# RMS norms of a two-block transformer step: the root read straight from PSUM, and residual additions alternating with the scaled products

## The chip, the cores and the metric

One NeuronCore of one Trainium2 chip runs the whole program. The metric is the device time in microseconds (us) of one execution, as the median of several. The engines are TensorE (PE, matrix products; PEld its weight loads), VectorE (DVE), ScalarE (ACT), GpSimd (POOL) and SyncE (SP, which issues the loads). They run their own instruction lists and meet at semaphores.

## The reference, cut to what matters

Two blocks follow one another on an activation of 256 tokens by 2048 channels in fp32. The first block is attention and a state-space mixer (SSM) side by side, an output projection, and a feed-forward part; the second is a linear-attention mixer (RWKV) and grouped attention, an output projection, and a layer of experts. All of them are joined by norms over the channels:

```python
def rms_norm(x, w):
    xf = x.astype(jnp.float32)
    y = xf * lax.rsqrt(jnp.mean(xf * xf, axis=-1, keepdims=True) + NORM_EPS)
    return (y * w.astype(jnp.float32)).astype(x.dtype)

# first block
h = rms_norm(x, ln_mix_pre[l])
...                                   # mixer; inside it two norms of 512 channels each
x = x + rms_norm(mixed, ln_mix_post[l])
h = rms_norm(x, ln_ffn_pre[l])
...
x = x + rms_norm(f, ln_ffn_post[l])
# second block
h = rmsnorm(x, norm1_w[l])
...
x = x + jnp.concatenate([y_rwkv, y_attn], axis=-1) @ w_out[l]
h2 = rmsnorm(x, norm2_w[l])
x = x + peer_ffn(h2, w_pq[l], sub_keys[l], u_tab[l], v_tab[l])
return rmsnorm(x, normf_w)
```

## The kernel before, in words

Activations lie with channels on the 128 partitions and the 256 tokens along the row, so 2048 channels are 16 tiles of 128x256. `xT` holds the residual stream, `acc` the output of a projection, `h_two` the normed activation as two fp32r parts (`h_hi`, `h_lo`). Weights come as panels of 128 output channels (1 MB) into `raw`; ScalarE copies them to `w_hi`, VectorE subtracts to get `w_lo`, and TensorE multiplies: `chunk` issues, for each of the 16 tiles of the sum, a product with `w_hi` (L502) and one with `w_lo` (L504). These weight streams fill nearly the whole program. Between two streams stands a norm, and no product of the next stream can start before it.

A norm goes through four engines' lists, by helpers that are called nine times, at the places `mix_pre`, `ssm` (two halves), `mix_post`, `ffn_pre`, `ffn_post`, `norm1`, `norm2`, `normf`:

- ScalarE, `squares` (L1098): squares four tiles at a time, in groups 0 to 3, into `quad[g % 2]`. Group g waits for its source, and from group 2 on for the sums of group g-2 (`sq_summed`), since there are two `quad` buffers.
- TensorE, `sums` (L525; L654 for the SSM halves): a matrix of ones sums the squares over the channels into `bank[2]` in PSUM, four matmuls for each group (the records show eight, for fp32 goes in two passes).
- VectorE, `rstd` (L1537, L1540): one TENSOR_SCALAR reads the bank and writes mean plus epsilon to `rb[0]` (`ms_done`); it then waits for the root and takes the reciprocal into `rb[0]`.
- ScalarE, `rms` (L1103): the square root, `rb[0]` to `rb[1]` (`rms_done`).
- After it either `normed` (L1555) on VectorE with `h_upper` (L1108) on ScalarE and `h_lower` (L1545) on VectorE make `h_two`, or `renew` on VectorE does the residual: 16 products `acc * weight * rb[0]` (L1566), then four additions of four tiles each to `xT` (L1571), each of which signals `x_new`. The squares of the following norm wait for `x_new` group by group.

So `mix_post` is followed at once by `ffn_pre`, and `ffn_post` by `norm1`: squares, sums, root, products, additions, and again squares, sums, root, products. Each engine runs its list strictly in the order written; nothing is planned by a scheduler. In the SSM norm, TensorE sums half 0, then half 1 into the same `bank[2]`, and before the second it waits for `ms_done`, that is until VectorE has read the first. VectorE treats half 0 completely (root, products, `h_lower`), then half 1. TensorE meanwhile begins the output projection, whose tiles 8 to 11 and 12 to 15 wait for the `h_lower` of the halves.

Of the kernel before, what the change touches and what calls it, by code (L numbers as in the profile page):

```python
# [13 lines left out]
P = 128  # L14
# [171 lines left out]
def build(nc, a, out):  # L186
    with ExitStack() as ctx:
        def sb(name, shape, dt=F32, at=ctx):
            return at.enter_context(nc.sbuf_tensor(name, shape, dt))

        def sem(name):
            return ctx.enter_context(nc.semaphore(name))
# [10 lines left out]
        stage = [sb(f"stage{j}", [P, T]) for j in range(2)]  # L203
        quad = [sb(f"quad{j}", [P, 4, T]) for j in range(2)]
        rb = [sb(f"rb{j}", [P, T]) for j in range(2)]


        part = ExitStack()
# [103 lines left out]
        copied, drained, acc_upper = sem("copied"), sem("bank_drained"), sem("acc_upper_added")  # L312
        stage_used = sem("stage_used")
        sq_ready, sq_summed = sem("squares_ready"), sem("squares_summed")
        ms_done, rms_done, rstd_done = sem("ms_done"), sem("rms_done"), sem("rstd_done")
        quad_ready, h_hi_done, h_lo_done = sem("quad_ready"), sem("h_hi_done"), sem("h_lo_done")
        x_new, acc_done = sem("x_renewed"), sem("acc_scaled")
        relb_loaded, toep_done, toep_copied, bias_in = (
# [170 lines left out]
        def _(pe):  # L489
# [159 lines left out]
            for g in range(2):  # L649
                pe.wait_ge(sq_ready, SQ["ssm"] + g + 1)  # L650
                if g == 1:
                    pe.wait_ge(ms_done, RS["ssm"] + 1)
                for k in range(4):
                    last = nc.tensor.matmul(bank[2][:, 0:T], ones, quad[g][:, k, :], start=(k == 0), stop=(k == 3))  # L654
                last.then_inc(sq_summed, 1)
# [408 lines left out]
        def _(act):  # L1064
# [28 lines left out]
            def squares(src, first, ready, groups=4):  # L1093
                for g in range(groups):
                    ready(g)
                    if g >= 2:
                        act.wait_ge(sq_summed, first + g - 1)
                    nc.scalar.activation(quad[g % 2][:], src[:, 4 * g:4 * g + 4, :], ACT.Square  # L1098
                                         ).then_inc(sq_ready, 1)

            def rms(i):
                act.wait_ge(ms_done, i + 1)
                nc.scalar.activation(rb[1][:], rb[0][:], ACT.Sqrt).then_inc(rms_done, 1)  # L1103

            def h_upper(first, groups=4, tile0=0):
                for g in range(groups):
# [2 lines left out]
                                         ).then_inc(h_hi_done, 1)  # L1109

            squares(xT, SQ["mix_pre"], lambda g: act.wait_ge(s_x, 64))
            split(0, 0)
            rms(RS["mix_pre"])
            h_upper(HG["mix_pre"])
            split(1, 0)
            for h in range(HEADS1):
# [57 lines left out]
                act.wait_ge(y_gated, 4 * g + 4)  # L1174
                nc.scalar.activation(quad[g][:], proj[:, 32 + 4 * g:36 + 4 * g, :], ACT.Square).then_inc(sq_ready, 1)
            for g in range(2):
                rms(RS["ssm"] + g)
                act.wait_ge(quad_ready, HG["ssm"] + g + 1)
                nc.scalar.activation(h_hi[:, 8 + 4 * g:12 + 4 * g, :], quad[g][:], ACT.Copy).then_inc(h_hi_done, 1)
            plain(N_OUT1, DT, acc)  # L1180
            squares(acc, SQ["mix_post"], lambda g: act.wait_ge(drained, N_OUT1 + 4 * g + 4))
            rms(RS["mix_post"])
            squares(xT, SQ["ffn_pre"], lambda g: act.wait_ge(x_new, XG["mix_post"] + g + 1))
            rms(RS["ffn_pre"])
            h_upper(HG["ffn_pre"])


# [29 lines left out]
                for j in range(2):  # L1217
                    split(c + DT + j, it0)
            squares(acc, SQ["ffn_post"], lambda g: act.wait_ge(drained, N_IN2))
            rms(RS["ffn_post"])  # L1220
            squares(xT, SQ["norm1"], lambda g: act.wait_ge(x_new, XG["ffn_post"] + g + 1))
            rms(RS["norm1"])
            h_upper(HG["norm1"])
            with act.Fori(0, 15) as i:
                for j in range(2):
# [155 lines left out]
                nc.scalar.activation(h_hi[:, 2 * p:2 * p + 2, :], quad[p % 2][:, 2:4, :], ACT.Copy).then_inc(gn_hi, 1)  # L1381
            plain(N_OUT2, DT, acc)
            squares(xT, SQ["norm2"], lambda g: act.wait_ge(x_new, XG["mix2"] + g + 1))
            rms(RS["norm2"])
            for g in range(4):
                act.wait_ge(quad_ready, HG["norm2"] + g + 1)
                nc.scalar.activation(h_hi[:, 4 * g:4 * g + 4, :], h_f32[:, 4 * g:4 * g + 4, :], ACT.Copy
# [72 lines left out]
                for j in range(2):  # L1460
                    split(N_PEER + DT + j + 2, (g + 1) * DT + i)
            squares(xT, SQ["normf"], lambda g: act.wait_ge(x_new, XG["peer"] + g + 1))
            rms(RS["normf"])

        @block.gpsimd
        def _(pool):

            nc.gpsimd.memset(relb[32:33, :], NEG).then_inc(relb_set, 1)
            for h in range(HEADS1):

                pool.wait_ge(toep_copied, h + 1)
                pool.dma_start(toep_d[h:h + 1, 0:P * 512].rearrange("a (p n) -> (a p) n", n=512), toep[h % 2][:]
                               ).then_inc(toep_out[h % 2], 16)
            for j in range(2):
                pool.wait_ge(toep_out[j], 16 * (HEADS1 // 2))
            for h in range(HEADS1):
                skew = toep_d[h:h + 1, P:P + P * 511].rearrange("a (p n) -> (a p) n", n=511)
                pool.dma_start(bias[:, h, :], skew[:, 0:T]).then_inc(bias_in, 16)

            pool.wait_ge(qk_done, 5)  # L1480
            pool.dma_start(k_swap[0:64, :, :], proj2[64:128, 38:40, :]).then_inc(k_swapped, 16)
            pool.dma_start(k_swap[64:128, :, :], proj2[0:64, 38:40, :]).then_inc(k_swapped, 16)

            pool.wait_ge(s3_done, 8)
            nc.gpsimd.memset(acc[:], 0.0).then_inc(acc_zero, 1)
            for b in range(T // 16):
                pool.wait_ge(gates_copied, 8 * (b + 1))
# [12 lines left out]
        def _(dve):  # L1500
# [31 lines left out]
                    for j in range(2):  # L1532
                        add_lower(n0 + count - 2 + j, c0 + count - 1 + j, dst[:, count - 2 + j, :])

            def rstd(i, squares_end, width):
                dve.wait_ge(sq_summed, squares_end)
                nc.vector.tensor_scalar(rb[0][:], bank[2][:, 0:T], 1.0 / width, EPS, ALU.mult, ALU.add  # L1537
                                        ).then_inc(ms_done, 1)
                dve.wait_ge(rms_done, i + 1)
                nc.vector.reciprocal(rb[0][:], rb[1][:]).then_inc(rstd_done, 1)  # L1540
                dve.wait_ge(rstd_done, i + 1)
# [20 lines left out]
            def renew(weight, scaled0):  # L1562

                for g in range(4):
                    for k in range(4):
                        last = nc.vector.scalar_tensor_tensor(acc[:, 4 * g + k, :], acc[:, 4 * g + k, :],  # L1566
                                                              pc(weight, 4 * g + k), rb[0][:], ALU.mult, ALU.mult)
                    last.then_inc(acc_done, 1)
                for g in range(4):
                    dve.wait_ge(acc_done, scaled0 + g + 1)  # L1570
                    nc.vector.tensor_tensor(xT[:, 4 * g:4 * g + 4, :], xT[:, 4 * g:4 * g + 4, :],  # L1571
                                            acc[:, 4 * g:4 * g + 4, :], ALU.add).then_inc(x_new, 1)

            dve.wait_ge(s_par, 16)
            dve.wait_ge(s_x, 64)
            rstd(RS["mix_pre"], SQ["mix_pre"] + 4, D)
            normed(HG["mix_pre"], "ln_mix_pre")
            lower(0, 0)
            lower(1, 0)
# [138 lines left out]
                                    ).then_inc(y_gated, 1)  # L1718
            dve.wait_ge(y_gated, 8)
            for g in range(2):  # L1720
                rstd(RS["ssm"] + g, SQ["ssm"] + g + 1, D // 4)
                dve.wait_ge(sq_summed, SQ["ssm"] + g + 1)
                for k in range(4):
                    last = nc.vector.scalar_tensor_tensor(quad[g][:, k, :], proj[:, 32 + 4 * g + k, :],
                                                          pc("ssm_norm_w", 4 * g + k), rb[0][:], ALU.mult, ALU.mult)
                last.then_inc(quad_ready, 1)
                h_lower(HG["ssm"] + g, quad[g][:], 8 + 4 * g)
            drain_to(acc, N_OUT1, C_OUT1, DT)
            rstd(RS["mix_post"], SQ["mix_post"] + 4, D)
            renew("ln_mix_post", 0)  # L1730
            rstd(RS["ffn_pre"], SQ["ffn_pre"] + 4, D)
            normed(HG["ffn_pre"], "ln_ffn_pre")


# [69 lines left out]
                    gather_down(i, FQT)  # L1804
                gather_down(DT // 2 - 1, DT)
            dve.wait_ge(drained, N_IN2)
            rstd(RS["ffn_post"], SQ["ffn_post"] + 4, D)
            renew("ln_ffn_post", 5)
            rstd(RS["norm1"], SQ["norm1"] + 4, D)
            normed(HG["norm1"], "norm1")  # L1810


# [315 lines left out]
            for g in range(4):  # L2128
                nc.vector.tensor_tensor(xT[:, 4 * g:4 * g + 4, :], xT[:, 4 * g:4 * g + 4, :],
                                        acc[:, 4 * g:4 * g + 4, :], ALU.add).then_inc(x_new, 1)  # L2130
            rstd(RS["norm2"], SQ["norm2"] + 4, D)
            for g in range(5):
                if g < 4:
                    for k in range(4):
# [168 lines left out]
            rstd(RS["normf"], SQ["normf"] + 4, D)  # L2303
            for g in range(4):
                if g >= 2:
                    dve.wait_ge(out_stored[g % 2], 16)
# [91 lines left out]
```

## Time and profile before

| | us |
|---|---|
| median of 3 runs | 3956.2 (3951.4 to 3966.77) |
| the profiled execution, time | 3949.75 |
| the profiled execution, span | 3948.1 |
| TensorE matmuls busy | 3589.8 (91%) |
| VectorE busy | 2446.9 (62%) |
| ScalarE busy | 1571.2 (40%) |

Mean granted TensorE clock over the span: 0.942 of full speed. Times in rows are us from the start of the span, durations marked "mean ns" are nanoseconds. A timeline row gives start, length, engine, line, operation, output<-inputs and, in brackets, how long the engine sat idle before it and what ended that. Rows of the same form that follow each other are merged, with their count behind the x. An engine idle for a time is free of charge unless it is on the chain that sets the end.

### The profile page before, as it was taken

The page shows a single profiled execution, that of the slowest core. Times are in us where ns is not written, and L with a number is a line of the kernel's source. Part 1 is how long each engine was busy: PE and PEld are TensorE (multiplying, and loading weights), DVE is VectorE, ACT ScalarE, POOL GpSimd, SP SyncE. Part 2 cuts the span into 40 slices and gives each one's busy share as a digit, 9 for nine tenths or more (in the row PEclk, how much of TensorE's full clock was granted, in tenths as well). Part 3 has the DMA queues.
Part 4 walks back from the last instruction along what each step waited for, and adds up shares of the span by engine and source line. Part 5 has one row for each costly group of instructions (what it writes and reads, how often), then busy time and mean ns, then how long its engine had stood idle before and what let it go on. Part 6 is the DMA issues. An engine that isn't in the chain of part 4 may idle for free.

```text
span 3948.1 us, 71481 instructions
## 1 busy us (share of the span) xinstructions
PE 3589.8 (91%) x24910; PEld 3057.9 (77%) x24910; DVE 2446.9 (62%) x4140; ACT 1571.2 (40%) x2433; POOL 32.7 (1%) x47
## 2 busy tenths in 40 slices
PE   6996979999999799568886898899999999999998
PEld 5884768888888688337775787688888888888887
DVE  3464567676767676536654559965656555565665
ACT  3433334444444344223322331443544444444543
POOL 0000000000000000000000000100000000000000
PEclk8996989999999999658998999999999999999999
DMA  4551225555555355000011453556656565656653
GB/s 171 187 182 43 100 102 182 190 174 195 173 195 173 130 187 192 23 6 13 8 35 39 142 167 122 174 180 211 212 181 213 184 213 185 212 182 212 202 189 130
DMA packets 165674, 593.36 MB, mean 150 GB/s; under 512 B 18432, under 2 KB 26752, under 8 KB 164288
## 3 DMA queue, kind: packets, MB, share of 16 engines
q1 hardware_dynamic: 159600, 559.10, 42.8%
q0 software_dynamic: 5968, 32.77, 2.3%
q8 instruction: 76, 1.25, 0.1%
q14 instruction: 30, 0.25, 0.0%
HBM read 572.66 MB, written 18.87 MB: 150 GB/s over the span
## 4 chain that ended last, share of the span: by engine, by line
PE 82%; DVE 12%; ACT 3%; issue 2%; DMA 1%; DVEq 0%; SPq 0%; ACTq 0%; POOL 0%; POOLq 0%
PE bank L502 46%; PE bank L504 24%; PE bank L754 5%; PE bank L525 2%; DVE hot_row L2234 1%; PE bank L742 1%; PE bank L716 1%; DVE hot_col L2229 1%; DVE quad L1555 1%; DVE proj L2003 0%; ACT w_hi L1070 0%; PE bank L732 0%; DVE q_ms L1865 0%; DVE h_two L1545 0%; DVE rb L1540 0%
## 5 line engine op out<-in xcount | busy, mean ns | idle before, releaser
L502 PE MATMUL bank<-h_two,w_hi 128*128 128x512 f32 x5616 | 1968.5, 395 | 44.2 <-DVE h_two L1545 30.3
L504 PE MATMUL bank<-h_two,w_lo 128*128 128x256 f32 x5616 | 1575.9, 281 | 0.0
L1505 DVE TENSOR_TENSOR w_lo<-raw,w_hi 128x1024 fp32r<-128x1024 f32 (+1 forms) x1054 | 1224.7, 1185 | 223.3 <-ACT w_hi L1070 217.8
L502 PEld LDWEIGHTS bank<-h_two,w_hi 128*128 128x128 f32 x5616 | 1057.7, 188 | 291.3 <-issue 37.9
L1070 ACT ACTIVATE w_hi<-raw 128x1024 fp32r<-128x1024 f32 (+1 forms) x1054 | 1045.2, 1025 | 562.7 <-PE bank L504 520.0
L504 PEld LDWEIGHTS bank<-h_two,w_lo 128*128 128x128 f32 x5616 | 1066.3, 190 | 0.0
L502 PE MATMUL bank<-p_two,w_hi 128*128 128x512 f32 x1792 | 631.0, 395 | 3.1 <-DVE acc L1523 1.9
L504 PE MATMUL bank<-p_two,w_lo 128*128 128x256 f32 x1792 | 500.7, 279 | 0.0
L502 PEld LDWEIGHTS bank<-p_two,w_hi 128*128 128x128 f32 x1792 | 336.5, 188 | 87.5 <-DVE p_two L2248 5.6
L504 PEld LDWEIGHTS bank<-p_two,w_lo 128*128 128x128 f32 x1792 | 336.5, 188 | 0.0
L1519 DVE TENSOR_TENSOR acc<-acc,bank 128x256 f32 x192 | 81.0, 422 | 393.2 <-PE bank L504 393.1
L1075 ACT ACTIVATE stage<-bank 128x256 f32<-128x256 f32 x242 | 93.0, 384 | 479.2 <-PE bank L504 478.8
L502 PE MATMUL bank<-f_two,w_hi 128*128 128x512 f32 x704 | 250.3, 397 | 12.0 <-DVE f_two L1771 12.0
L1515 DVE TENSOR_TENSOR stage<-stage,bank 128x256 f32<-128x256 f32 x242 | 101.9, 421 | 206.7 <-ACT stage L1075 206.5
L504 PE MATMUL bank<-f_two,w_lo 128*128 128x256 f32 x704 | 200.6, 285 | 0.0
L502 PEld LDWEIGHTS bank<-f_two,w_hi 128*128 128x128 f32 x704 | 134.8, 192 | 41.8 <-DVE f_two L1771 13.2
L504 PEld LDWEIGHTS bank<-f_two,w_lo 128*128 128x128 f32 x704 | 135.9, 193 | 0.0
L999 PE MATMUL bank<-h_f,raw 128*128 128x256 f32 x512 | 120.5, 381 | 0.0
L525 PE MATMUL bank<-quad,cst 128*128 128x256 f32 x224 | 62.9, 450 | 50.7 <-ACT quad L1098 50.7
L999 PEld LDWEIGHTS bank<-h_f,raw 128*128 128x128 f32 x512 | 93.6, 192 | 10.4
L525 PEld LDWEIGHTS bank<-quad,cst 128*128 128x128 f32 x224 | 51.0, 231 | 61.9 <-ACT quad L1098 41.1
L1036 PEld LDWEIGHTS bank<-hot_row,hot_col 128*128 128x128 f32 x512 | 68.0, 206 | 38.2 <-DVE hot_row L2234 35.1
(328 smaller groups left out, 2850.6 us busy)
## 6 DMA issues: line engine op xcount, KB each, us to landing
raw<-in_u_tab SPq DMA_DIRECT2D x256, 512.0 KB, 4.0
raw<-in_v_tab SPq DMA_DIRECT2D x256, 512.0 KB, 4.5
raw<-in_w_up SPq DMA_DIRECT2D x176, 512.0 KB, 4.8
raw<-in_w_in SPq DMA_DIRECT2D x174, 512.0 KB, 4.3
raw<-in_w_out SPq DMA_DIRECT2D x64, 512.0 KB, 4.5
raw<-in_w_down SPq DMA_DIRECT2D x64, 512.0 KB, 3.5
raw<-in_w_pq SPq DMA_DIRECT2D x32, 512.0 KB, 4.4
gates<-g_stage POOLq DMA_DIRECT2D x16, 896.0 KB, 5.3
```

The source lines that it names most:

```text
L502: nc.tensor.matmul(o[:], wh, two[:, k, :, :].rearrange("p a t -> p (a t)"), start=(k == 0), stop=False)
L504: last = nc.tensor.matmul(o[:, T:2 * T], wl, two[:, k, 0, :], start=False, stop=(k == nk - 1))
L525: last = nc.tensor.matmul(bank[2][:, 0:T], ones, quad[g % 2][:, k, :], start=(g == 0 and k == 0), stop=(g == groups - 1 and k == 3))
L716: last = nc.tensor.matmul(bank[3 + qh % 2][:, tt * T:(tt + 1) * T], proj2[r:r + 64, 30 + m, tt * P:(tt + 1) * P], k_t, start=True, stop=True)
L754: return nc.tensor.matmul(o, lhs, rhs, start=start, stop=stop)
L999: last = nc.tensor.matmul(bank[c % 2][:, 0:T], raw[c % 2][:, k * P:(k + 1) * P], h_f32[:, k, :], start=(k == 0), stop=(k == DT - 1))
L1036: last = nc.tensor.matmul(bank[3 + n % 2][:, x * P:(x + 1) * P], hot_col[n % 2][:, x, :], hot_row[n % 2][:, x, :], start=True, stop=True)
L1070: nc.scalar.activation(w_hi[c % 2][:, at:end], raw[c % 2][:, at:end], ACT.Copy).then_inc(hi_done, 1)
L1075: nc.scalar.activation(dst, bank[c % 2][:, 0:T], ACT.Copy).then_inc(copied, 1)
L1505: nc.vector.tensor_tensor(w_lo[c % 2][:, at:end], raw[c % 2][:, at:end], w_hi[c % 2][:, at:end].bitcast(F32), ALU.subtract).then_inc(lo_do ...
L1515: nc.vector.tensor_tensor(dst, dst, bank[c % 2][:, T:2 * T], ALU.add).then_inc(drained, 1)
L1519: nc.vector.tensor_tensor(dst, dst, bank[c % 2][:, 0:T], ALU.add).then_inc(acc_upper, 1)
```

## The change

ScalarE takes the root from PSUM with `scale=1/width` and `bias=eps`, where `eps` is a new tile of 128x1, filled once by GpSimd at the start. VectorE's TENSOR_SCALAR goes, and `ms_done` with it. ScalarE now waits for the sums itself, and for the previous reciprocal, which read `rb[1]`. TensorE's wait in the SSM norm is for the root of half 0 instead of its mean. In `renew` the addition of a group follows the four products of that group. The other calls change in their arguments alone.

```diff
+        eps = sb("eps", [P, 1])
...
                 if g == 1:
-                    pe.wait_ge(ms_done, RS["ssm"] + 1)
+                    pe.wait_ge(rms_done, RS["ssm"] + 1)
...
-            def rms(i):
-                act.wait_ge(ms_done, i + 1)
-                nc.scalar.activation(rb[1][:], rb[0][:], ACT.Sqrt).then_inc(rms_done, 1)
+            def rms(i, squares_end, width=D):
+
+                act.wait_ge(sq_summed, squares_end)
+                if i:
+                    act.wait_ge(rstd_done, i)
+                nc.scalar.activation(rb[1][:], bank[2][:, 0:T], ACT.Sqrt, scale=1.0 / width, bias=eps[:]
+                                     ).then_inc(rms_done, 1)
...
             squares(xT, SQ["mix_pre"], lambda g: act.wait_ge(s_x, 64))
+            act.wait_ge(eps_set, 1)
             split(0, 0)
-            rms(RS["mix_pre"])
+            rms(RS["mix_pre"], SQ["mix_pre"] + 4)
...
         def _(pool):
 
+            nc.gpsimd.memset(eps[:], EPS).then_inc(eps_set, 1)
+            pool.wait_ge(eps_set, 1)
             nc.gpsimd.memset(relb[32:33, :], NEG).then_inc(relb_set, 1)
...
-            def rstd(i, squares_end, width):
-                dve.wait_ge(sq_summed, squares_end)
-                nc.vector.tensor_scalar(rb[0][:], bank[2][:, 0:T], 1.0 / width, EPS, ALU.mult, ALU.add
-                                        ).then_inc(ms_done, 1)
+            def rstd(i):
                 dve.wait_ge(rms_done, i + 1)
                 nc.vector.reciprocal(rb[0][:], rb[1][:]).then_inc(rstd_done, 1)
                 dve.wait_ge(rstd_done, i + 1)
...
                     last.then_inc(acc_done, 1)
-                for g in range(4):
                     dve.wait_ge(acc_done, scaled0 + g + 1)
                     nc.vector.tensor_tensor(xT[:, 4 * g:4 * g + 4, :], xT[:, 4 * g:4 * g + 4, :],
                                             acc[:, 4 * g:4 * g + 4, :], ALU.add).then_inc(x_new, 1)
...
             for g in range(2):
-                rstd(RS["ssm"] + g, SQ["ssm"] + g + 1, D // 4)
-                dve.wait_ge(sq_summed, SQ["ssm"] + g + 1)
+                rstd(RS["ssm"] + g)
```

## Rows read from the trace of the kernel before

**Rows 1.** The page: busy time of PE, and the chain that ended last.
```profile
PE 3589.8 (91%) x24910; PEld 3057.9 (77%) x24910; DVE 2446.9 (62%) x4140; ACT 1571.2 (40%) x2433; POOL 32.7 (1%) x47
PE 82%; DVE 12%; ACT 3%; issue 2%; DMA 1%; DVEq 0%; SPq 0%; ACTq 0%; POOL 0%; POOLq 0%
```
**Rows 2.** Timeline from mix_post's root to ffn_pre's: start, us, engine, line, operation.
```profile
535.17 0.42 DVE L1537 TENSOR_SCALAR rb<-bank 128x256 f32<-128x256 f32 x1 [9.37 <-PE bank L525]
535.63 0.42 ACT L1103 ACTIVATE rb<-rb 128x256 f32<-128x256 f32 x1 [2.80 <-DVE rb L1537]
536.08 1.75 DVE L1540 RECIPROCAL rb<-rb 128x256 f32<-128x256 f32 x1 [0.48 <-ACT rb L1103]
537.86 6.42 DVE L1566 SCALAR_TENSOR_TENSOR acc<-acc,par,rb 128x256 f32<-128x256 f32 x16
544.20 4.63 DVE L1571 TENSOR_TENSOR xT<-xT,acc 128x1024 f32<-128x1024 f32 x4
545.46 2.20 ACT L1098 ACTIVATE quad<-xT 128x1024 f32<-128x1024 f32 x2 [9.41 <-DVE xT L1571]
...
546.57 9.41 PE L525 MATMUL bank<-quad,cst 128*128 128x256 f32 x32 [11.44 <-ACT quad L1098]
550.45 1.06 ACT L1098 ACTIVATE quad<-xT 128x1024 f32<-128x1024 f32 x1 [2.80 <-PE bank L525]
...
556.02 0.42 DVE L1537 TENSOR_SCALAR rb<-bank 128x256 f32<-128x256 f32 x1 [7.19 <-PE bank L525]
```
**Rows 3.** Granted clock: us from:to, busy of PE, PEld, DVE, ACT, POOL, PEclk, DMA.
```profile
548.50:550.50 2.00, 2.00 (x6) 1.63 (x5) 0.33 (x1) 0.05 (x1) 0.00 (x0) 0.50 0.00 0
552.50:554.50 2.00, 2.00 (x11) 1.77 (x10) 0.00 (x0) 1.06 (x1) 0.00 (x0) 1.00 0.00 0
```
**Rows 4.** Timeline of ffn_post and norm1, the same two norms again.
```profile
1325.33 1.28 ACT L1103 ACT_TABLE_LOAD   x1
1327.74 0.42 DVE L1537 TENSOR_SCALAR rb<-bank 128x256 f32<-128x256 f32 x1 [7.30 <-PE bank L525]
...
1336.77 4.62 DVE L1571 TENSOR_TENSOR xT<-xT,acc 128x1024 f32<-128x1024 f32 x4
...
1348.25 0.42 DVE L1537 TENSOR_SCALAR rb<-bank 128x256 f32<-128x256 f32 x1 [6.86 <-PE bank L525]
```
**Rows 5.** Timeline of the norm in the SSM, in two halves.
```profile
416.61 1.99 PE L654 MATMUL bank<-quad,cst 128*128 128x256 f32 x8
...
418.71 0.42 DVE L1537 TENSOR_SCALAR rb<-bank 128x256 f32<-128x256 f32 x1 [1.05 <-PE bank L654]
418.76 1.28 ACT L1103 ACT_TABLE_LOAD   x1
...
419.28 1.97 PE L654 MATMUL bank<-quad,cst 128*128 128x256 f32 x8 [0.68 <-DVE rb L1537]
...
426.23 0.42 DVE L1537 TENSOR_SCALAR rb<-bank 128x256 f32<-128x256 f32 x1
...
426.46 0.47 PE L502 MATMUL bank<-h_two,w_hi 128*128 128x512 f32 x1 [2.44 <-DVE h_two L1545]
...
427.13 1.75 DVE L1540 RECIPROCAL rb<-rb 128x256 f32<-128x256 f32 x1 [0.48 <-ACT rb L1103]
```
**Rows 6.** The first norm, mix_pre, on ScalarE.
```profile
20.23 1.28 ACT L1103 ACT_TABLE_LOAD   x1
...
21.52 0.42 ACT L1103 ACTIVATE rb<-rb 128x256 f32<-128x256 f32 x1
```
**Rows 7.** The nine roots: duration ns min/median/max, first and last start.
```profile
L1103 ACT ACTIVATE rb<-rb x9: 416/416/418, 21.5 to 3935.0; 128x256 f32<-128x256 f32 x9
```
**Rows 8.** Groups by line and form in 1765 to 1850 us: busy us, mean ns.
```profile
L1291 ACT ACTIVATE sig_a<-bank,small 128x256 f32<-128x256 f32 x6 | 2.5, 471 | 8.5 <-PE bank L765 8.5
```
**Rows 9.** The page's costliest groups: products on the tiles that lie behind `eps`.
```profile
L502 PE MATMUL bank<-p_two,w_hi 128*128 128x512 f32 x1792 | 631.0, 395 | 3.1 <-DVE acc L1523 1.9
...
L502 PE MATMUL bank<-f_two,w_hi 128*128 128x512 f32 x704 | 250.3, 397 | 12.0 <-DVE f_two L1771 12.0
```

More of the change, by code:

```diff
@@ L314, in build @@
         sq_ready, sq_summed = sem("squares_ready"), sem("squares_summed")
[L315 removed]
+        eps_set, rms_done, rstd_done = sem("eps_set"), sem("rms_done"), sem("rstd_done")
         quad_ready, h_hi_done, h_lo_done = sem("quad_ready"), sem("h_hi_done"), sem("h_lo_done")
@@ L1176, in _ @@
             for g in range(2):
-                rms(RS["ssm"] + g)
+                rms(RS["ssm"] + g, SQ["ssm"] + g + 1, D // 4)
                 act.wait_ge(quad_ready, HG["ssm"] + g + 1)
@@ L1181, in _ @@
             squares(acc, SQ["mix_post"], lambda g: act.wait_ge(drained, N_OUT1 + 4 * g + 4))
-            rms(RS["mix_post"])
+            rms(RS["mix_post"], SQ["mix_post"] + 4)
             squares(xT, SQ["ffn_pre"], lambda g: act.wait_ge(x_new, XG["mix_post"] + g + 1))
-            rms(RS["ffn_pre"])
+            rms(RS["ffn_pre"], SQ["ffn_pre"] + 4)
             h_upper(HG["ffn_pre"])
@@ L1219, in _ @@
             squares(acc, SQ["ffn_post"], lambda g: act.wait_ge(drained, N_IN2))
-            rms(RS["ffn_post"])
+            rms(RS["ffn_post"], SQ["ffn_post"] + 4)
             squares(xT, SQ["norm1"], lambda g: act.wait_ge(x_new, XG["ffn_post"] + g + 1))
-            rms(RS["norm1"])
+            rms(RS["norm1"], SQ["norm1"] + 4)
             h_upper(HG["norm1"])
@@ L1383, in _ @@
             squares(xT, SQ["norm2"], lambda g: act.wait_ge(x_new, XG["mix2"] + g + 1))
-            rms(RS["norm2"])
+            rms(RS["norm2"], SQ["norm2"] + 4)
             for g in range(4):
@@ L1462, in _ @@
             squares(xT, SQ["normf"], lambda g: act.wait_ge(x_new, XG["peer"] + g + 1))
-            rms(RS["normf"])
+            rms(RS["normf"], SQ["normf"] + 4)
         @block.gpsimd
         def _(pool):
+            nc.gpsimd.memset(eps[:], EPS).then_inc(eps_set, 1)
+            pool.wait_ge(eps_set, 1)
             nc.gpsimd.memset(relb[32:33, :], NEG).then_inc(relb_set, 1)
@@ L1575, in _ @@
             dve.wait_ge(s_x, 64)
-            rstd(RS["mix_pre"], SQ["mix_pre"] + 4, D)
+            rstd(RS["mix_pre"])
             normed(HG["mix_pre"], "ln_mix_pre")
@@ L1728, in _ @@
             drain_to(acc, N_OUT1, C_OUT1, DT)
-            rstd(RS["mix_post"], SQ["mix_post"] + 4, D)
+            rstd(RS["mix_post"])
             renew("ln_mix_post", 0)
-            rstd(RS["ffn_pre"], SQ["ffn_pre"] + 4, D)
+            rstd(RS["ffn_pre"])
             normed(HG["ffn_pre"], "ln_ffn_pre")
@@ L1806, in _ @@
             dve.wait_ge(drained, N_IN2)
-            rstd(RS["ffn_post"], SQ["ffn_post"] + 4, D)
+            rstd(RS["ffn_post"])
             renew("ln_ffn_post", 5)
-            rstd(RS["norm1"], SQ["norm1"] + 4, D)
+            rstd(RS["norm1"])
             normed(HG["norm1"], "norm1")
@@ L2130, in _ @@
                                         acc[:, 4 * g:4 * g + 4, :], ALU.add).then_inc(x_new, 1)
-            rstd(RS["norm2"], SQ["norm2"] + 4, D)
+            rstd(RS["norm2"])
             for g in range(5):
@@ L2302, in _ @@
                                         acc[:, 4 * g:4 * g + 4, :], ALU.add).then_inc(x_new, 1)
-            rstd(RS["normf"], SQ["normf"] + 4, D)
+            rstd(RS["normf"])
             for g in range(4):
```

## The prediction

> **What bounds the kernel now.** I read the page's busy times and its chain first. TensorE is busy 91% of the span and holds 82% of the chain that ended last; VectorE has 12% and ScalarE 3% [rows 1]. So the time is set by weight streams, and nothing that the change edits lies inside a stream. What it edits are the nine norms between the streams, where TensorE waits and VectorE, ScalarE and TensorE hand one tile to and fro. The second view is therefore the timeline of one such stretch, from the root of mix_post to that of ffn_pre [rows 2]. The reader is to see that it is one serial chain: each engine's idle time in brackets is ended by the engine before it in the chain, so each step taken out there should come off the total. The third view is the granted clock in that stretch [rows 3], because TensorE has idled 11.44 us before these sums. The fourth is the same timeline at the second pair of norms [rows 4], in the SSM [rows 5] and at the start [rows 6], because a table load or another queue may be the later of two waits there.
>
> **The root read straight from PSUM, at six plain norms** (mix_post, ffn_pre, ffn_post, norm1, norm2, normf). Removed: VectorE's operation that turns sums into mean plus epsilon. From its start to the start of the root it is 535.63 - 535.17 = 0.46 us [rows 2]. Added: the root now reads PSUM, takes a scale and a bias tile. The root takes 416 ns in all nine places [rows 7]. The nearest row to the new form is a Tanh of the same 128x256, from PSUM, with a scale and a bias tile: 471 ns [rows 8]. I take that: 55 ns more. The gain is 0.46 - 0.055 = 0.405 us each, six times 2.43 us. Bounds: at 416 ns it is 0.46 each, 2.8 in all. Whether ScalarE wakes as fast after TensorE as VectorE did no row here separates; VectorE took 418.71 - 418.60 = 0.11 us after the end of the sums [rows 5], and if ScalarE took twice that, the gain would be 0.3 each, 1.8 in all.
>
> The Trainium skill, in "ScalarE: Activation LUTs", section "What ACT_TABLE_LOAD costs", speaks against this edit: it says that a 128x1 pointer operand adds about 93 ns to an ACTIVATE. An estimate by that page, for six norms, would be 0.46 - 0.093 = 0.37 each and 2.2 in all. The Tanh row's 55 ns over the root is on the cheaper side of it; they differ in source as well, so it doesn't settle the rule.
>
> ScalarE's table load for the root must not be uncovered by this. At ffn_post it runs from 1325.33 to 1326.61 while ScalarE waits, and VectorE's operation begins only at 1327.74 [rows 4]; normf has the same order. The load is 1.13 us early, so the root can start at the end of the sums.
>
> **mix_pre.** Here the load is the later one: it begins at 20.23, ends at 21.51, and the root starts at 21.52 [rows 6], long after the sums. Taking VectorE's operation away gives nothing, and the root is 0.055 longer: -0.06 us. GpSimd's fill of `eps` is queued ahead of its first fill of `relb`, at the very start, 20 us before the root needs it; the copy of weights that waits for it comes after three rounds of squares and sums. I cost both at nothing; the cover is these 20 us.
>
> **The SSM norm.** Half 0: ScalarE's load, 418.76 to 420.04, ends after VectorE's operation (418.71 + 0.42 = 419.13) [rows 5], so here too the root starts when it did; the 0.055 that it is longer stays. TensorE's sums of half 1 began at 419.28, right after VectorE had read the bank; now they wait for the end of the root, about 420.05 + 0.47 = 420.52, so they come 1.24 us later. Queued behind them on TensorE are tiles 0 to 7 of the output projection. But tile 8 sat idle for 2.44 us before it started, for `h_lower` of half 0 [rows 5]. 1.24 of these 2.44 are eaten and 1.2 are left: cost nothing, with the cover named; without it the cost would be 1.24. Half 1: VectorE read the bank at 426.23, only after it was through with half 0, and the reciprocal came at 427.13. Now ScalarE makes the second root while VectorE is in `h_lower`, since nothing else is queued on it there, and the reciprocal follows `h_lower` directly: 427.13 - 426.23 = 0.90 us less 0.06 from half 0, so 0.84 us. That is on the path, for tiles 12 to 15 wait for it.
>
> Together: 2.43 - 0.06 + 0.84 = 3.21 us.
>
> **Residual additions between the products.** Before, the 16 products run from 537.86, then the four additions from 544.20 to 544.20 + 4.63 = 548.83. The first `x_new` thus comes late, the squares start at 545.46, and TensorE's four groups of sums follow each other until 556.02 [rows 2]. They are slow at first: from the start at 546.57 to the square that the first group released at 550.45 it is 3.88 us, at granted clock 0.50, the lower of the two levels (1.2 GHz); later it is 1.00 (2.4 GHz) [rows 3]. After the change the first group's products end at about 537.86 + 6.42/4 + 0.06 = 539.5, its addition at 540.8, its square at 541.9, and TensorE starts at 541.9 instead of 546.57. The low-clock groups then run beside VectorE's remaining products and additions, one group every 2.8 us or so. What is late next is VectorE's last addition. VectorE does the same work plus four waits for its own result. Such a wait costs the overlap of two operations, 537.86 + 6.42 - 544.20 = 0.08, and the handoff, 537.86 - (536.08 + 1.75) = 0.03 [rows 2]: 0.11 each, 0.44 in all. So the last addition ends at 549.27; 0.04 later its square, which takes 1.06, 0.05 to TensorE, and then one group of sums from rest at full clock, 418.71 - 416.61 = 2.10 us to the next engine's start [rows 5]: 552.52. Against 556.02 that is 3.50 us.
>
> At the second place the same sum gives 1336.77 + 4.62 + 0.44 + 0.04 + 1.06 + 0.05 + 2.10 = 1345.08 against 1348.25 [rows 4]: 3.17 us. Both: 6.67 us. This rests on the clock having risen by the last group. In rows 3 it rose 4 to 6 us after the sums had begun; that would be at 546 to 548 now, before the last square's end at 550.4. norm2 and normf have additions without products, so nothing is gained there but the root.
>
> **Sum.** 3.21 + 6.67 = 9.9 us, from 3949.75 to 3939.9 for the profiled execution, 0.25%. That execution is 6.5 us below the median of the runs shown, 3956.2; I take the gain off the median: 3946.3 us.
>
> **The rivals.** (a) The clock doesn't rise in time, and TensorE's sums become the bound of the interleaved stretch. At the low level four groups take 4 x 3.88 = 15.5 us from 541.9, to 557.4, which is 1.4 us later than before; likewise at the second place from about 1334.5 to 1350.0, 1.8 us later. The time would be 3956.2 - 3.2 + 3.2 = 3956. For it: these sums start after long idleness and come in pieces. Against: at the low clock a group takes 3.88 us and VectorE delivers one every 2.8, so TensorE would have no pause, and in the same sums before it rose after 4 to 6 us.
>
> (b) The root's table load slips behind the wait for the sums, because the root now has two waits. It is then uncovered at ffn_post and normf: 2 x 1.28 = 2.6 us, so 3948.9. Against: of two waits the added one, for the last reciprocal, was met long before. The Trainium skill, same page and section, says that a switch costs another 1380 ns of drain; an estimate by it would be 5.3 us for the two loads. The trace doesn't show that drain: the root starts 0.01 us after the load's end [rows 6].
>
> (c) Slower: `eps` is placed ahead of all tiles of the later parts, so `f_two`, `p_two`, `acc` and others move to other addresses. If reads from the new ones are slower, the long streams pay. The products on these two tiles that are in the rows sum to 631.0 + 250.3 = 881.3 us [rows 9]. They decide against the change from 9.9/881.3 = 1.1% on, 4.4 ns of each 395; at 13 ns more each (3.4%) it is 30 - 9.9 = 20 us slower, 3976. For it: nothing in the trace. Against: 395 and 397 ns on two tiles that lie at different places.
>
> (d) The change doesn't do what it says: the additions alternate but squares still go one by one behind TensorE; that is (a) in effect.
>
> **How the numbers follow.** Chances: forecast 0.76, (a) with its milder forms 0.10, (b) 0.08, (c) 0.04, something else 0.02. The unknown costs (0.3 to 0.46 a norm, the group of sums at either clock, 1 us of clock phase at each of three stream starts) give 6 to 12 us of gain. The three runs lie 15 us apart, so a median can be off by some 8. The range: 3936 to 3960. Over 0.5% (19.8 us), about what a measurement of this kernel can tell from no change, is twice the forecast gain: faster 0.06, within 0.89, slower 0.05.
>
> **What would show it.** In the changed kernel: a root of about 471 ns, with VectorE's L1537 gone; the reciprocal some 0.9 us earlier in SSM half 1; TensorE's sums of ffn_pre and norm1 starting 4 to 5 us earlier relative to the products and the root there following 3 to 3.5 us earlier; the streams with unchanged durations. It would be wrong if these sums end at the low clock, if a table load stands between the sums and the root, or if L502 changes its mean.

## The result, and the profile after

The changed kernel is slower, by 0.22%: ratio to the kernel before 1.0022, 95% interval 1.0012 to 1.0032, medians 3963.74 and 3955.07 us over 22 runs each. The forecast was 3946.3 with a range up to 3960; the time is 3.7 us above it, and on the other side of the kernel before. The profiled execution took 3954.64 us (span 3952.8).

The norms did what was forecast. The timeline of VectorE from mix_post's reciprocal to ffn_pre's, which answers [rows 2]:

```profile
529.35 1.75 DVE L1545 RECIPROCAL rb<-rb 128x256 f32<-128x256 f32 x1 [9.92 <-ACT rb L1107]
531.14 1.67 DVE L1571 SCALAR_TENSOR_TENSOR acc<-acc,par,rb 128x256 f32<-128x256 f32 x4
532.85 1.23 DVE L1575 TENSOR_TENSOR xT<-xT,acc 128x1024 f32<-128x1024 f32 x1
533.99 1.67 DVE L1571 SCALAR_TENSOR_TENSOR acc<-acc,par,rb 128x256 f32<-128x256 f32 x4
...
541.38 1.23 DVE L1575 TENSOR_TENSOR xT<-xT,acc 128x1024 f32<-128x1024 f32 x1
546.28 1.75 DVE L1545 RECIPROCAL rb<-rb 128x256 f32<-128x256 f32 x1 [3.68 <-ACT rb L1107]
```

Products and additions alternate, and from reciprocal to reciprocal it is 546.28 - 529.35 = 16.93 us, against 556.02 - 535.17 = 20.85 before [rows 2]. ScalarE and TensorE in the same stretch:

```profile
528.85 0.47 ACT L1107 ACTIVATE rb<-bank,eps 128x256 f32<-128x256 f32 x1 [2.34 <-PE bank L526]
534.11 1.06 ACT L1099 ACTIVATE quad<-xT 128x1024 f32<-128x1024 f32 x1 [4.79 <-DVE xT L1575]
...
542.64 1.06 ACT L1099 ACTIVATE quad<-xT 128x1024 f32<-128x1024 f32 x1 [1.78 <-DVE xT L1575]
545.78 0.47 ACT L1107 ACTIVATE rb<-bank,eps 128x256 f32<-128x256 f32 x1 [2.08 <-PE bank L526]
```
```profile
535.22 5.10 PE L526 MATMUL bank<-quad,cst 128*128 128x256 f32 x16 [6.41 <-ACT quad L1099]
540.91 1.99 PE L526 MATMUL bank<-quad,cst 128*128 128x256 f32 x8 [0.59 <-ACT quad L1099]
543.75 1.99 PE L526 MATMUL bank<-quad,cst 128*128 128x256 f32 x8 [0.85 <-ACT quad L1099]
```

The last two groups of sums wait for ScalarE, which waits for VectorE's addition: so VectorE's additions now set the time of this stretch. The clock, us from:to with PEclk (granted share of the full clock) behind POOL's busy time, rose some 3 us after the sums had begun:

```profile
536.00:538.00 2.00, 2.00 (x7) 1.53 (x6) 2.00 (x4) 1.05 (x1) 0.00 (x0) 0.50 0.00 0
538.00:540.00 2.00, 2.00 (x11) 1.71 (x9) 1.97 (x4) 0.22 (x2) 0.00 (x0) 0.99 0.00 0
```

Where did the time go? The start of the same matmul in both traces, taken every 250 matmuls, tells where they drift apart. After less before, in us: 0.0 at 90 us; -4.1 at the end of the first stream (312 us); -6.4 before mix_post; -10.55 after ffn_pre; -2.4 at the end of the feed-forward part; -6.3 after norm1 and up to norm2; -4.1 where the expert part's first p_two stream begins (2672 us); **+7.5** at its end; +5.1 at the last matmul, behind `normf`. So the norms gave what they should, and the long weight streams, where the change edits nothing, took some 8 us in the feed-forward part and 12 in the expert part. Of the 2.4 us that `normf` gave back, the root is only 0.4; its 32 sums, which the change leaves alone, ran in 7.17 us at a granted clock of 1.00, and in 10.03 us at first at 0.50 in the kernel before, which is luck of these two executions. The sums of `normf`, before and after:

```profile
3924.52 10.03 PE L525 MATMUL bank<-quad,cst 128*128 128x256 f32 x32 [3.32 <-ACT quad L1098]
```
```profile
3932.46 7.17 PE L526 MATMUL bank<-quad,cst 128*128 128x256 f32 x32 [3.32 <-ACT quad L1099]
```

The groups of the page, answering [rows 1] and [rows 9]:

```profile
PE 3606.0 (91%) x24910; PEld 3060.4 (77%) x24910; DVE 2443.8 (62%) x4131; ACT 1572.2 (40%) x2433; POOL 32.8 (1%) x48
...
L503 PE MATMUL bank<-h_two,w_hi 128*128 128x512 f32 x5616 | 1981.5, 398 | 39.3 <-DVE h_two L1550 25.1
...
L503 PE MATMUL bank<-p_two,w_hi 128*128 128x512 f32 x1792 | 631.4, 394 | 2.8 <-DVE acc L1531 1.7
...
L503 PE MATMUL bank<-f_two,w_hi 128*128 128x512 f32 x704 | 256.4, 405 | 11.8 <-DVE f_two L1774 11.8
```

TensorE has the same 24910 matmuls and is busy 16.2 us longer. The products on `f_two` grew from 250.3 to 256.4. The page's mean mixes stream starts at the low clock with the middle of the stream, so I cut windows inside streams: groups by form in 100 to 200 us (`h_two`), 890 to 930 (`f_two`) and 2780 to 2820 (`h_two` between two `p_two` streams). First the kernel before, then the changed one:

```profile
L502 PE MATMUL bank<-h_two,w_hi 128*128 128x512 f32 x284 | 100.4, 399 | 0.0
...
L502 PE MATMUL bank<-f_two,w_hi 128*128 128x512 f32 x117 | 40.6, 390 | 0.0
...
L502 PE MATMUL bank<-h_two,w_hi 128*128 128x512 f32 x116 | 40.3, 391 | 0.0
```
```profile
L503 PE MATMUL bank<-h_two,w_hi 128*128 128x512 f32 x290 | 100.6, 391 | 0.0
...
L503 PE MATMUL bank<-f_two,w_hi 128*128 128x512 f32 x114 | 40.3, 396 | 0.0
...
L503 PE MATMUL bank<-h_two,w_hi 128*128 128x512 f32 x114 | 40.3, 399 | 0.0
```

The reader is to see two paces of the same instruction at the same full clock (granted 1.00 in all six windows): 290 against 284 pairs of products in 100 us. From start to start within a stream a pair (one product with `w_hi`, one with `w_lo`) on `h_two` takes 346.7 ns or 353.3 ns, 1.9% apart, and it keeps one of them for a whole stream. Over all 8112 pairs that would be worth some 53 us. Of the streams compared here, the kernel before had the slow pace in the first one, the changed kernel in all four passes over `f_two` and in all eight `h_two` streams of the expert part. (The last of these eight holds the final group's expert values, which the kernel writes into `h_two`.)

It isn't a collision with the other engines' accesses. In the slow first stream of the kernel before, from 100 to 300 us, three pairs in a row always take 1060 ns: in 17 such triples during which ScalarE and VectorE were both busy for less than a tenth of the time as in 11 during which both were for more than nine tenths, and in 5 with no DMA under way as in 148 with more than twenty.

### The profile page after: what moved, and what is told of

Its sections match the earlier page's. It is cut to its first block, busy times and chain, and to the rows that moved or that the text cites. A ratio compares the mean times of both kernels' runs of the same rounds, so it can differ in the third digit from the quotient of the medians.

```text
span 3952.8 us, 71480 instructions
## 1 busy us (share of the span) xinstructions
PE 3606.0 (91%) x24910; PEld 3060.4 (77%) x24910; DVE 2443.8 (62%) x4131; ACT 1572.2 (40%) x2433; POOL 32.8 (1%) x48
## 4 chain that ended last, share of the span: by engine, by line
PE 82%; DVE 12%; ACT 3%; issue 2%; DMA 1%; DVEq 0%; SPq 0%; ACTq 0%; POOL 0%; POOLq 0%
PE bank L503 47%; PE bank L505 24%; PE bank L755 5%; DVE hot_row L2237 1%; PE bank L526 1%; PE bank L743 1%; PE bank L717 1%; DVE hot_col L2232 1%; DVE proj L2006 0%; PE bank L733 0%; ACT w_hi L1071 0%; DVE quad L1560 0%; DVE q_ms L1868 0%; DVE rb L1545 0%; PE bank L1037 0%
## 5 line engine op out<-in xcount | busy, mean ns | idle before, releaser
L503 PE MATMUL bank<-f_two,w_hi 128*128 128x512 f32 x704 | 256.4, 405 | 11.8 <-DVE f_two L1774 11.8
L1442 ACT ACTIVATE u_act<-stage 128x256 f32 x112 | 46.8, 418 | 124.7 <-DVE p_raw L2245 124.7
```

The source lines that it names most:

```text
L503: nc.tensor.matmul(o[:], wh, two[:, k, :, :].rearrange("p a t -> p (a t)"), start=(k == 0), stop=False)
L1442: nc.scalar.activation(tile_of(u_act, i * 2 + j), stage[j][:], ACT.Gelu).then_inc(gelu_done, 1)
```

## The experiments

Theory A: the pace depends on where the tiles lie. Tiles are allocated at multiples of 32 bytes, so `eps`, 4 bytes a partition, had pushed `proj`, `acc`, `f_two`, `p_two` and all else behind it 32 bytes on. Theory B: each stream falls into a pace by chance, so the 0.22% is bad luck in many draws. Places below are bytes past a multiple of 128, with the weight buffers at 0 unless said otherwise; a tile of `h_two`, `f_two` or `p_two` is 2048 bytes from the next, so the whole stream has the same place. The places are worked out from the order and sizes of the tiles in each kernel; the traces hold no addresses. Before: `h_two` 0, `f_two` 32, `p_two` 96. Changed: 0, 64, 0. A pace without a fence is the mean distance from start to start, in ns a pair, over that tile's streams in the trace.

**x1, one unused tile in the kernel before.**
```diff
         rb = [sb(f"rb{j}", [P, T]) for j in range(2)]
+        sb("pad", [P, 1])
```


> The kernel before with one unused tile of 128x1 ahead of the later parts, nothing else, so that proj, acc, f_two, p_two and the rest start 32 bytes further on. Theory A (addresses set the pace of the streams): products on f_two take the slow pace, 353.3 ns for a pair of products instead of 346.7, those on p_two some 352 instead of 351, and the h_two streams between the p_two streams turn slow as well; together about 4.7 + 2.0 + 12.7 = 19 us, ratio 1.004 to 1.005. Theory B (each stream falls into one of the two paces by chance at its start, whatever the addresses): ratio 0.999 to 1.001, and the paces of this profile are another mixture.

Measured: 1.0039 [1.0026, 1.0052], median 3975.07. `f_two` 353.3 in three of four passes, 349.1 in the last; `p_two` 351.1; all `h_two` streams between them 353.3, as theory A had it. An unused tile, with no instruction, costs more than the whole change. Windows 2700 to 2740 and 2780 to 2820:
```profile
L503 PE MATMUL bank<-p_two,w_hi 128*128 128x512 f32 x115 | 40.4, 393 | 0.0
...
L503 PE MATMUL bank<-h_two,w_hi 128*128 128x512 f32 x115 | 40.7, 399 | 0.0
```

**x2, the changed kernel with no tile moved.**
```diff
-        par = sb("par", [P, NPAR])
+        par_eps = sb("par", [P, NPAR + 1])
+        par, eps = par_eps[:, 0:NPAR], par_eps[:, NPAR:NPAR + 1]
-        eps = sb("eps", [P, 1])
```


> The changed kernel with eps in a spare column behind the parameters, so that no tile moves against the kernel before. Theory A: the gain of the norms stays alone, ratio 0.997 to 0.998 (about -10 us), and f_two at 346.7 ns a pair. Theory B: as the changed kernel, 1.001 to 1.003. Theory C (the changed order itself costs it somewhere in the streams): also 1.001 to 1.003, with f_two slow in places.

Measured: 0.9969 [0.9956, 0.9982], median 3943.21, which is 3.1 us below the forecast's 3946.3. `f_two` 346.8 to 347.4. Of the expert part's eight `h_two` streams the first, at 2565 us, ran at 353.3, the seven behind a `p_two` stream at 346.7. Windows 890 to 930 and 2780 to 2820:
```profile
L503 PE MATMUL bank<-f_two,w_hi 128*128 128x512 f32 x117 | 40.6, 390 | 0.0
...
L503 PE MATMUL bank<-h_two,w_hi 128*128 128x512 f32 x117 | 40.6, 391 | 0.0
```
x1 and x2 speak for A and against B as the cause of the 0.22%.

**x3, the kernel before with `h_two` at 32.**
```diff
+        sb("pad0", [P, 1])
         h_two = sb("h_two", [P, DT, 2, T], F32R)
+        sb("pad1", [P, 1])
```


> The kernel before with h_two moved by 32 bytes and everything from proj on by 64, so that h_two too starts at 32 bytes past a multiple of 64, as f_two and p_two do in the kernel before. Theory A in its simplest form (32 past a multiple of 64 is the fast place): all h_two streams at 346.7 ns a pair, ratio 0.998 to 1.0. Theory B: 0.999 to 1.001 with a mixture of paces.

Measured: 0.9972 [0.996, 0.9984], 3946.12, a little more gain than the 0.998 to 1.0 expected. All `h_two` streams at 346.7; `p_two`, which came to 32 by this, 346.7 too; `f_two`, which came to 96, 350.3. So it isn't the place within 64 bytes that counts, as I had written, but within 128: 32 and 96 differ.

**x4, the changed kernel again.** No edit.

> The changed kernel once more, for the repeat of its paces. Theory A: f_two slow in all four passes and the streams from 2660 us on slow, as in its first profile; ratio 1.002. Theory B: another mixture of paces.

Measured: 1.0013 [1.0002, 1.0024]. `f_two` at 353 in all passes, as the first time. Of the expert part's `h_two` streams the seven behind a `p_two` stream ran at 353.3 again, but the first, at 2574 us, at 346.7. And the streams of norm1 (672 pairs) and of the output projection behind it (256 pairs) ran at 353.3 this time and 346.7 the first: with `h_two` at 0 part of it is chance, as B says.

**x5, every moving tile at 32, in the changed kernel.**
```diff
+        sb("pad0", [P, 8])
         h_two = sb("h_two", [P, DT, 2, T], F32R)
+        sb("pad1", [P, 24])
...
         slot_T = sb("slot_T", [P, 3, T], at=part)
+        sb("pad2", [P, 16], at=part)
```
(on x2.)

> The changed kernel with eps in the spare column, and unused tiles that place h_two, f_two and p_two all at 32 bytes past a multiple of 128, the place at which every stream seen so far ran at 346.7 ns a pair. Theory A (addresses): all streams at 346.7; from the kernel before that is about -10 us of the norms, -6.4 us on the first h_two streams, -5.9 us on p_two (1792 pairs, 350.0 to 346.7): ratio 0.993 to 0.9955. Theory B (chance): as the run with tiles left in place, 0.9965 to 0.9975.

Measured: 0.9937 [0.9922, 0.9953], median 3929.45, the fastest kernel here. Every stream runs at 346.7 to 346.8. TensorE's busy time fell from 3606.0 to
```profile
PE 3574.5 (91%) x24910; PEld 3069.3 (78%) x24910; DVE 2444.1 (62%) x4131; ACT 1571.5 (40%) x2433; POOL 32.8 (1%) x48
```
Its six runs lie within 5.1 us (3926.06 to 3931.12), the 23 of the kernel before on the same chip within 19.8 (3945.11 to 3964.86). That would fit a draw of paces in the one and none in the other, but the same kernel's next six runs (x10) lie 14.9 us apart, one of them at 3938.66 and the others within 5.7, so the spread proves little.

**x6 and x7, the two parts of the change alone**, no tile moved.
```diff
 # x6, on the kernel before
                     last.then_inc(acc_done, 1)
-                for g in range(4):
                     dve.wait_ge(acc_done, scaled0 + g + 1)
 # x7, on x2
                     last.then_inc(acc_done, 1)
+                for g in range(4):
                     dve.wait_ge(acc_done, scaled0 + g + 1)
```


> The kernel before with only the additions put between the products. From mix_post's reciprocal to ffn_pre's it takes 20.85 us before and 16.93 in the changed kernel; theory of the forecast: the order alone brings it to 17.3 (0.4 more than the whole change, for the root), TensorE's sums start 4 to 5 us earlier; ratio 0.998 to 0.9987. Rival (VectorE's waits for its own results cost more than 0.11 each, or the clock stays low): over 18.5, ratio 0.999 or more.

> The kernel before with only the root from PSUM, eps in the spare column, additions behind all products as before. Forecast: 0.4 us off each of six norms, 0.84 us off the SSM norm, 3.2 us in all, ratio 0.999 to 0.9995; from mix_post's reciprocal to ffn_pre's 20.45 us. Rival (the root from PSUM saves nothing): 20.85 and ratio 1.0.

Measured: x6 0.9988 [0.9974, 1.0002], x7 0.9993 [0.9979, 1.0006]. Neither interval excludes 1, and both fit the forecast; with `h_two` at 0 the paces' draw hides gains of this size. The traces are sharper. VectorE from root to root in x6, then in x7:
```profile
535.65 1.75 DVE L1540 RECIPROCAL rb<-rb 128x256 f32<-128x256 f32 x1 [0.48 <-ACT rb L1103]
...
552.98 1.75 DVE L1540 RECIPROCAL rb<-rb 128x256 f32<-128x256 f32 x1 [0.48 <-ACT rb L1103]
```
```profile
526.34 1.75 DVE L1545 RECIPROCAL rb<-rb 128x256 f32<-128x256 f32 x1 [8.82 <-ACT rb L1107]
...
546.46 1.75 DVE L1545 RECIPROCAL rb<-rb 128x256 f32<-128x256 f32 x1 [7.36 <-ACT rb L1107]
```
x6: 17.33 us, expected 17.3. x7: 20.12, expected 20.45, and the missing 0.3 is in the sums, whose 32 matmuls took 9.08 us instead of 9.41 [rows 2] because the clock rose sooner, some 3.9 us after their start instead of 4.6. The gains of the two parts, 3.52 and 0.73 us, add up to 4.25, the whole change gave 3.92; they agree but for that 0.3.

**x8, the kernel before with `h_two` at 64**, the others where they were within 128 bytes.
```diff
+        sb("pad0", [P, 16])
         h_two = sb("h_two", [P, DT, 2, T], F32R)
+        sb("pad1", [P, 16])
```

> The kernel before with h_two at 64 bytes past a multiple of 128; f_two and p_two keep their places within 128 bytes. If the place within 128 bytes sets the pace for h_two as it did for f_two (353.1 ns at 64), the h_two streams are at 353; if only the place within 64 counts, they fall into 346.7 or 353.3 as they do at 0.

Measured: 3975.44 in one run, beside 3956.03. `h_two` never at 346.7: 349 or 353.3. `f_two`, at 32, ran at 346.7 to 347.0 between them. `p_two`, at 96 as in the kernel before, ran at 353.3 in six streams and at 346.7 in one, where it had had 350.0. So 128 bytes don't say it all. Taken within 256 bytes, `p_two` has moved here, from 96 to 224.

**x9 and x10, the change by itself with the paces held.** x9 is the kernel before with the pads of x5; x10 is x5 again, on the same chip.
```diff
 # x9, on the kernel before
+        sb("pad0", [P, 8])
         h_two = sb("h_two", [P, DT, 2, T], F32R)
+        sb("pad1", [P, 24])
...
+        sb("pad2", [P, 16], at=part)
```

> The kernel before, with h_two, f_two and p_two at 32 bytes past a multiple of 128 as in the best kernel, and nothing else changed. Theory A: all streams at 346.7, 12.3 us less than the kernel before in its first profile: ratio 0.996 to 0.9975. The best kernel over this one is then the change by itself with the paces held: 0.9970 to 0.9978 (9 to 12 us). Rival (the change gains nothing but lucky paces): both at the same time.

> The best kernel again, on the same chip as the kernel before with placed tiles: ratio 0.993 to 0.9955 to the kernel before, all streams at 346.7 again if addresses decide, a mixture if chance does.

Measured: x9 0.9963 [0.995, 0.9977], 3939.99; x10 0.9935 [0.9919, 0.9951], 3927.71. All streams of both at 346.7 to 347.4. The change is thus worth 3939.99 - 3927.71 = 12.3 us by the medians of six runs each (a ratio of 0.9969, where 0.9970 to 0.9978 was expected), 9.8 us by the profiled spans (3936.3 and 3926.5); the forecast was 9.9.

**x11 and x12, one tile each moved away from 32**, on x5.
```diff
 # x11: f_two to 64
+        sb("pad3", [P, 8], at=part)
         f_two = sb("f_two", [P, FQT, 2, T], F32R, at=part)
 # x12: p_two (and u_act, g_now with it) to 0
-        sb("pad2", [P, 16], at=part)
+        sb("pad2", [P, 8], at=part)
```


> The best kernel with f_two alone moved to 64 bytes past a multiple of 128, its place in the changed kernel. Theory A: only the f_two streams slow, 353 a pair, 704 x 6.6 ns = 4.6 us. Rival (a slow f_two drags the h_two streams behind it): h_two after f_two slow too.

> The best kernel with the expert part's tiles from u_act on moved so that p_two starts at a multiple of 128, its place in the changed kernel; h_two stays well placed. If h_two's slow pace between the p_two streams in the changed kernel was inherited from p_two but needs h_two's own place at 0 as well: p_two at 351, h_two at 346.7. If it is inherited regardless: h_two at 353.3 too, some 15 us in all.

Measured, one run each: 3933.01 and 3933.38. x11: `f_two` 353.2 to 353.4, everything else 346.7, and 4.7 us more than x10's profiled run, for 4.6 expected. The rival (a slow `f_two` drags `h_two`) falls for an `h_two` at 32. For one at 0 the changed kernel, x1 and x4 answer it: of the nine `h_two` streams that follow a slow `f_two` stream there, eight ran at 346.7. x12: `p_two` at 353.3 in four streams and at 347.0 in three; `h_two` 346.7 throughout. The 351 expected for `p_two` was missed: it had been at 0 within 128 bytes in the changed kernel as well, but at 128 within 256, and is at 0 within 256 here. So in the changed kernel the expert part's `h_two` could be slow behind `p_two` only because it lay at 0 itself. Windows of x11 at 890 to 930 and of x12 at 2700 to 2740 and 2780 to 2820:
```profile
L507 PE MATMUL bank<-f_two,w_hi 128*128 128x512 f32 x112 | 39.6, 397 | 0.0
```
```profile
L506 PE MATMUL bank<-p_two,w_hi 128*128 128x512 f32 x115 | 40.7, 399 | 0.0
...
L506 PE MATMUL bank<-h_two,w_hi 128*128 128x512 f32 x116 | 40.3, 390 | 0.0
```

**x13 and x14, weights moved too.** So far the weight buffers lay at 0 in every kernel, so a tile's place and its distance from the weights were the same number.
```diff
 # both, on x5
+        sb("pad_w", [P, 8])
         raw = [sb(f"raw{j}", [P, PW]) for j in range(2)]
 # x13 alone: keeps the moving tiles at 32; x14 has them at 64
-        sb("pad0", [P, 8])
```


> The best kernel with the weight buffers (raw, w_hi, w_lo) moved by 32 bytes as well, so that weights and moving tiles both start at 32 past a multiple of 128, where before the weights were at 0. Absolute theory (the moving tile's own address counts): all streams at 346.7 ns a pair, 3925 to 3930 us. Relative theory (the distance between moving tile and weights counts, 32 being the fast one): as at distance 0, p_two slow at 351 or more and h_two at 346.7 or 353.3, 3935 to 3955 us.

> Weights at 32 and h_two, f_two, p_two at 64 past a multiple of 128, so the distance is 32 again. Absolute theory: f_two at 353.1 as in the changed kernel, h_two 349 to 353.3 as in the run with h_two at 64, 3950 to 3975 us. Relative theory: all streams at 346.7, 3925 to 3930 us.

Measured: x13 3948.79, x14 3930.63, one run each. x13, with the moving tiles at 32 and distance 0, is no longer fast: `f_two` 351, `h_two` and `p_two` at either pace. x14, which is x5 with all tiles 32 bytes further on, has the moving tiles at 64, where they were slowest, and yet has every stream at 346.7 to 346.8, because the distance is 32. The absolute theory falls in both, the relative one holds in both (x14 is 0.6 us above its 3925 to 3930). The weights' three kinds of buffer, `raw`, `w_hi` and `w_lo`, moved together, and `xT` with them, so which of them counts isn't shown. Windows 2700 to 2735 and 2780 to 2820, x13 and then x14:
```profile
L506 PE MATMUL bank<-p_two,w_hi 128*128 128x512 f32 x101 | 35.7, 399 | 0.0
...
L506 PE MATMUL bank<-h_two,w_hi 128*128 128x512 f32 x114 | 40.3, 399 | 0.0
```
```profile
L507 PE MATMUL bank<-p_two,w_hi 128*128 128x512 f32 x102 | 35.4, 390 | 0.0
...
L507 PE MATMUL bank<-h_two,w_hi 128*128 128x512 f32 x117 | 40.6, 390 | 0.0
```

## Why the prediction was right or wrong, point by point

**The root, six norms: right.** The root takes 473 ns (median of nine) where 471 was taken from the Tanh row, and VectorE's operation is gone. The reciprocal of norm2 comes 15.26 us after the stream's last product, 15.67 before: 0.41 for a forecast 0.405. The Trainium skill's 93 ns for a 128x1 operand ("ScalarE: Activation LUTs", section "What ACT_TABLE_LOAD costs") isn't borne out as a sum here: 473 - 416 = 57 ns, with the source changed from SBUF to PSUM at the same time, so the operand alone remains unmeasured.

**The table load, rival (b): it stayed covered.** At ffn_post, ScalarE:
```profile
1323.07 1.28 ACT L1107 ACT_TABLE_LOAD   x1
1325.39 0.47 ACT L1107 ACTIVATE rb<-bank,eps 128x256 f32<-128x256 f32 x1 [1.04 <-PE bank L526]
```
The load ends at 1324.35, and ScalarE still waits 1.04 us for the sums.

**The SSM norm: the gain right, the cover gone where it was sought.** ScalarE, VectorE and TensorE in the changed kernel:
```profile
414.41 0.47 ACT L1107 ACTIVATE rb<-bank,eps 128x256 f32<-128x256 f32 x1
...
419.44 0.46 ACT L1107 ACTIVATE rb<-bank,eps 128x256 f32<-128x256 f32 x1
```
```profile
414.98 1.75 DVE L1545 RECIPROCAL rb<-rb 128x256 f32<-128x256 f32 x1 [2.98 <-ACT rb L1107]
...
420.71 1.75 DVE L1545 RECIPROCAL rb<-rb 128x256 f32<-128x256 f32 x1
```
```profile
410.96 1.99 PE L655 MATMUL bank<-quad,cst 128*128 128x256 f32 x8
415.03 3.62 PE L655 MATMUL bank<-quad,cst 128*128 128x256 f32 x8 [2.08 <-ACT rb L1107]
...
426.57 0.79 PE L503 MATMUL bank<-h_two,w_hi 128*128 128x512 f32 x1 [3.73 <-DVE h_two L1550]
```
And tile 12 in the kernel before:
```profile
432.99 0.79 PE L502 MATMUL bank<-h_two,w_hi 128*128 128x512 f32 x1 [4.89 <-DVE h_two L1545]
```
The second root runs beside `h_lower`, and the reciprocals are 5.73 us apart; before, from 420.50 to 427.13, 6.63. That is 0.90 less. From the start of the first sums to tile 12 it was 432.99 - 416.61 = 16.38 us and is 426.57 - 410.96 = 15.61, so the gain is 0.77 for a forecast 0.84. TensorE's sums of half 1 wait for the first root as written. They also run at the low clock for most of their time (3.62 us for 1.97 before [rows 5]), which I hadn't forecast. With that the 1.2 us of cover that I had left before tile 8 are gone: tile 8 no longer waits for `h_lower` of half 0, it comes 0.49 us after its end (421.29 after 420.80). This costs nothing only because tile 12 has a wait of its own, 4.89 us before and 3.73 now, which I hadn't named.

**The additions between the products: right.** From reciprocal to reciprocal, 20.85 to 16.93 is 3.92 us (forecast 3.50 + 0.41), at the second place 20.52 to 16.93, 3.59 (forecast 3.17 + 0.41). The clock rose in time, so rival (a) is out, and (d) with it.

**Rival (c): this is what happened, and its weighing is the step that failed.** I gave it 0.04 on the ground that the products on `f_two` and `p_two` show 397 and 395 ns at different places [rows 9]. Both numbers were read wrongly. They are means of a group with stream starts in it, those at the low clock on `f_two`, behind 12.0 us of idling, among them. Inside the streams the kernel before shows 390 for `f_two` (window above) and 393 for `p_two`, here from 2700 to 2740 us:
```profile
L502 PE MATMUL bank<-p_two,w_hi 128*128 128x512 f32 x116 | 40.6, 393 | 0.0
```
That is a difference by place, 346.7 and 350.0 a pair. (The mean of these rows isn't the pace either: x1 has 393 here at 351.1 a pair.) The 881.3 us were also the products with `w_hi` alone; those with `w_lo` on the same tiles, another 500.7 + 200.6 us by the page, were left out. And I priced only the streams on tiles that move, and put the others at nothing without a reason. The larger part came from `h_two`, which doesn't move: the seven expert streams behind a `p_two` stream, 1792 pairs, at 353.3 instead of 346.7, 11.8 us, against 704 x 6.6 = 4.6 us on `f_two` and 1792 x 1.1 = 2.0 us on `p_two`. With the 9.9 us of the norms off, that is +8.5 us; the medians of 22 runs say +8.7, and a match so close is partly luck, for the other `h_two` streams draw their pace anew in each execution. The first profile pair alone shows less (+4.7 us by the spans), because the kernel before had drawn the slow pace in its first 720 pairs and the changed one the fast (4.8 us), and because of the clock in `normf`.

**The range.** It was made of 6 to 12 us of gain and some 8 us of chance in a median; a loss in the streams, the largest part of the program, had no room in it at all.

## What to carry to other kernels

A new tile moves every tile allocated after it, and that alone cost more than the edit gave: between the changed kernel (x4) and the same with no tile moved (x2) lie 18.3 us, against the edit's 10 to 12. Put small new tiles behind the rest or into a spare column, and compare kernels with the streams' operands held in place. Before reading a change of a fraction of a per cent, take the pace inside the long streams, from start to start, not the mean of the group, and do it in both traces. A serial chain between streams can be forecast to tenths of a us from the timeline; the streams beside it have to be checked, not assumed.

## What the runs showed of the hardware

Back-to-back fp32r products on TensorE, 128x512 and 128x256 by turns with weights loaded for each, run at a pace that goes with the distance of the moving tile from the weight buffers in SBUF. Modulo 128 bytes, as the experiments were planned, it leaves x8 and x12 unexplained; modulo 256 all runs fall into place:

| distance mod 256 | ns a pair | where |
|---|---|---|
| 32, 160 | 346.7, up to 347.4 with stream starts | all tiles in x5, x9, x10, x14; `f_two` in before, x2, x6, x7, x8, x12; `p_two` in x3, x11; `h_two` in x3, x11, x12 |
| 96 | 350.0 to 350.4 | `p_two` in before, x2, x6, x7; `f_two` in x3 |
| 224 | 353.3 in six streams, 346.7 in one | `p_two` in x8 |
| 64, 192 | 353.1 to 353.4; 349 or 353.3 | `f_two` in after, x4, x11 and, one pass at 349, x1; `h_two` in x8 |
| 128 | 351.1 | `p_two` in after, x1, x4; `f_two` in x13 |
| 0 | 346.7 or 353.3, one for a whole stream (`p_two` 347.0 or 353.3) | `h_two` in before, after, x1, x2, x4, x6, x7, x13; `p_two` in x12, x13 |

The modulus of 256 was found in runs made for something else; no run was planned to test it.

At distance 0 a stream that begins behind a pause takes either pace, and one that follows another stream at once goes by that stream. `h_two` at 0 ran at 346.7 in all 28 streams behind `p_two` at 96 and all 12 behind `f_two` at 32 (before, x2, x6, x7), and in 8 of 9 behind `f_two` at 64; it ran at 353.3 in all 21 behind `p_two` at 128 (after, x1, x4). In x13 it was slow behind each of six slow streams and fast behind each of four fast ones. So moving `p_two` slowed `h_two`, which lay still. What in the chip makes the difference no run here shows; distances other than multiples of 32 weren't tried, nor other shapes. x8 and x11 to x14 were run once each.
